# A recurrent mixer by chunks of 64 tokens with affine maps of the state, instead of chunks of 128 with a three-product chain

## The reference

```python
def wkv7_scan(r, w, k, v, a, b):
    def step(state, inp):
        r_t, w_t, k_t, v_t, a_t, b_t = inp
        sa = jnp.einsum('bhvk,bhk->bhv', state, a_t)
        state = (state * w_t[:, :, None, :] + sa[..., None] * b_t[:, :, None, :]
                 + v_t[..., None] * k_t[:, :, None, :])
        return state, jnp.einsum('bhvk,bhk->bhv', state, r_t)
...
    y = wkv7_scan(rh, wh, kh, vh, -kk, kk * ah)
    mu = jnp.mean(y, axis=-1, keepdims=True)
    var = jnp.mean(jnp.square(y - mu), axis=-1, keepdims=True)
    y = ((y - mu) * lax.rsqrt(var + GN_EPS)).reshape(B, S, C) * gn_w + gn_b
```

## Time and profile before

| | |
|---|---|
| median of 3 runs | 3302.31 us (3301.39 to 3302.34) |
| profiled execution, its own time | 3304.38 us |
| its span | 3302.4 us |
| PE, DVE, ACT, POOL busy | 96%, 52%, 32%, 60% |
| recurrent section | from about 243 to 783 us |
| mean distance of passes 1 to 7 (first products of round 1) | 60.8 us |

### The profile page before, as it was taken

How to read it: one execution, slowest core, us unless ns; L and a number is a source line. 1 busy time by engine, 2 the same in 40 slices (tenths; PEclk the granted TensorE clock), 3 DMA queues, 4 the chain that set the end, 5 groups by cost and what they waited for, 6 DMA issues and landing times.

```text
span 3302.4 us, 54354 instructions
## 1 busy us (share of the span) xinstructions
PE 3173.8 (96%) x19314; PEld 2521.1 (76%) x19314; DVE 1703.5 (52%) x2741; ACT 1066.7 (32%) x1988; POOL 1972.7 (60%) x2607
## 2 busy tenths in 40 slices
PE   6998999999999999899999999999999999999999
PEld 4766777777888888577778888887667777888887
DVE  4456777765554335542645554446551635565345
ACT  2153434432221113542635321113552535331112
POOL 4624333336588885246465888886327373898886
PEclk8999999999999999999999999999999999999999
DMA  5341111112233232112121322232102121223322
GB/s 210 138 163 51 46 40 40 40 34 77 93 98 100 95 96 65 32 52 83 40 82 58 96 96 96 95 96 83 45 27 95 46 83 46 93 93 100 98 95 96
DMA packets 70794, 265.22 MB, mean 80 GB/s; under 512 B 7744, under 2 KB 7872, under 8 KB 67520
## 3 DMA queue, kind: packets, MB, share of 16 engines
q1 hardware_dynamic: 68288, 257.59, 23.7%
q10 hardware_dynamic: 2304, 4.83, 0.4%
HBM read 260.29 MB, written 2.10 MB: 79 GB/s over the span
## 4 chain that ended last, share of the span: by engine, by line
PE 83%; DVE 9%; ACT 5%; issue 1%; DMA 1%; SPq 0%; DVEq 0%; ACTq 0%
PE psum_a L579 10%; PE psum_a L583 10%; PE psum_a L582 10%; PE psum_d L579 7%; PE psum_d L583 6%; PE psum_d L582 6%; PE psum_d L645 5%; PE psum_a L737 3%; PE psum_d L840 2%; PE psum_a L767 2%; PE psum_a L771 2%; PE psum_a L770 2%; PE psum_a L608 1%; PE psum_a L611 1%; PE psum_a L612 1%
## 5 line engine op out<-in xcount | busy, mean ns | idle before, releaser
L3383 POOL TENSOR_TENSOR w_lo<-raw,w_hi 128x256 fp32r<-128x256 f32 x1736 | 1425.7, 852 | 36.3
L3377 POOL TENSOR_TENSOR mark<-mark 128x1 f32<-128x1 f32 x432 | 105.2, 244 | 1248.0 <-PE psum_a L579 627.7
L579 PE MATMUL psum_a<-h_hi,w_hi 128*128 128x512 f32 x1600 | 631.9, 395 | 0.0
L583 PE MATMUL psum_a<-h_hi,w_lo 128*128 128x512 f32 x1600 | 623.7, 390 | 0.0
L582 PE MATMUL psum_a<-h_lo,w_hi 128*128 128x512 f32 x1600 | 623.3, 390 | 0.0
L3378 POOL TENSOR_SCALAR w_hi<-raw 128x1024 fp32r<-128x1024 f32 x434 | 459.6, 1059 | 33.3 <-DMA raw<-in_weights 33.3
L579 PEld LDWEIGHTS psum_a<-h_hi,w_hi 128*128 128x128 f32 x1600 | 300.8, 188 | 71.7 <-issue 10.7
L582 PEld LDWEIGHTS psum_a<-h_lo,w_hi 128*128 128x128 f32 x1600 | 300.9, 188 | 63.2 <-issue 2.2
L583 PEld LDWEIGHTS psum_a<-h_hi,w_lo 128*128 128x128 f32 x1600 | 300.7, 188 | 63.2
L579 PE MATMUL psum_d<-split,w_hi 128*128 128x512 f32 x848 | 329.9, 389 | 0.0
L582 PE MATMUL psum_d<-split,w_hi 128*128 128x512 f32 x848 | 329.9, 389 | 0.0
(11 more groups left out here) (407 smaller groups left out, 5524.7 us busy)
## 6 DMA issues: line engine op xcount, KB each, us to landing
raw<-in_weights SPq DMA_DIRECT2D x434, 512.0 KB, 3.4
plain<-in_ada SPq DMA_DIRECT2D x20, 1024.0 KB, 6.9
arena<-in_ada SPq DMA_DIRECT2D x4, 1024.0 KB, 16.9
x<-in_x SPq DMA_DIRECT2D x1, 2048.0 KB, 12.2
x<-in_x ACTq DMA_DIRECT2D x1, 2048.0 KB, 9.9
out<-x SPq DMA_DIRECT2D x8, 256.0 KB, 3.5
arena<-in_pe ACTq DMA_DIRECT2D x2, 512.0 KB, 3.6
const<-in_const ACTq DMA_DIRECT2D x1, 906.0 KB, 8.5
```

Source lines behind the costliest of these rows:

```text
L579: m = pe.eng.matmul(dst, wh, hi(t), start=t == 0, stop=False)
L583: m = pe.eng.matmul(dst, wl, hi(t), start=False, stop=t == k - 1)
L3377: eng.tensor_tensor(b.mark[:, 1:2], b.mark[:, 0:1], b.mark[:, 0:1], ALU.add)
L3383: m = eng.tensor_tensor(lo[:, part], b.raw[:, s, part], hi[:, part].bitcast(F32), ALU.subtract)
```

## The change

Chunks become 64 tokens, eight per head; there is no step from 64 to 128 tokens. Per chunk the state update becomes an affine map S' = E(P S + Q), and the output R' S + Y0; P, Q, R' and Y0 don't depend on the state and are made for all chunks at once. In PE's order:

- `inputs` between g2 and gate: 16 products of 128 columns (inverse times A and times K·V), copied by ACT. `maps` between gate and branch: one group of 16 products of 128 columns, two groups of 32 products of 64 columns (two terms each). DVE makes P, R' and Q (`dve_rwkv_transitions`), ACT copies Y0.
- `pe_rwkv_start` and the halves become two `pe_units` groups of 16 64-column products, masks of 256 columns instead of 512.
- The chain is six `step`s of two 64x64x64 products, two each in rounds 1 to 3, each followed by one DVE operation of 64 columns. In round 4 `outputs`: 14 products of 64 columns, and on DVE an addition of 448 columns and a copy of 64.
- The tail has the transposes, one group of 16 products of 64 columns (B, R), one of 128 columns (K, A and R), copies of A by 16 products with the identity, four transposes of the inverse, and a group of 16 (K·V). The maps' masks are two of 256 and two of 512 columns.
- The turned values go to ring "d"; DVE reduces them over the channels (8 sums per token row) and subtracts the mean while it takes them (`dve_rwkv_values`). The product for the mean of y (`pe_rwkv_mean`) and DVE's centring go.
- The log decay is one scan over 512 tokens, reset by a zero in a vector of ones at each chunk's start, and no middle is subtracted: two exponentials of 512 columns instead of eight of 128 and two small ones. Three memsets prepare the constants.
- After pass 7: gate, `inputs`, gate, `maps`, two gates with three steps each, `outputs`, gate, variance. Gates 3 to 6 go to ring "a" and are taken by ACT with the sigmoid, without DVE's copy.

The core of the diff:

```diff
-    pe_rwkv_start(pe, lambda r, c: b.R_BH[r, c * P:(c + 1) * P], lambda r, c: AR[r, c, 0])
...
+    if chain:
+        chain.inputs()
     pe_features(pe, "a", "gate", H)
+    if chain:
+        chain.maps()
     pe_features(pe, "d", "branch", of(b.s_hi, b.s_lo, 2), 2)
     pe.eng.wait_ge(pe.sem["rk_ready"], pe.due("rk_ready"))
     pe_plain(pe, "d", b.pair, b.R_T)
+    pe_units(pe, "d", (B, A))
+    pe_units(pe, "d", (A, B))
...
+        if chain and k <= 3:
+            chain.step(2 * k - 1)
+        if chain and k == 4:
+            chain.outputs()
...
-        if k == 5:
-            if j:
-                pe_rwkv_mean(pe)
-        if c is not None:
-            chain.second(c)
...
+        normal = pe_units(pe, "d", (block(b.R_TW), block(b.R_Z)))
+        if chain and k <= 3:
+            chain.step(2 * k)
         if k == 3 and more:
             pe_rwkv_length(pe)
...
+    pe_turned(pe, [b.R_V[:, q * P:(q + 1) * P] for q in range(NQ)], "d")
+    for src in (b.R_BH, b.R_KH):
+        turned = pe_turned(pe, [src[:, q * P:(q + 1) * P] for q in range(NQ)])
+    pe_units(pe, "d", (B, R))
+    maps = pe_units(pe, "d", (K, lambda v, row, out: AR[ROWS[row], 2 * v + out]), width=P)
+    pe_own_rows(pe, "a", lambda r, c: AR[r, c, 0], lambda r, c: b.ident[r, r], range(8))
     pe.eng.wait_ge(normal.free, pe.taken(normal))
...
+    inverse = pe_turned(pe, [b.R_TN[:, 2 * v:2 * v + 2].rearrange("p u t -> p (u t)") for v in range(4)])
+    pe.eng.wait_ge(turned.free, pe.taken(turned))
+    pe.eng.wait_ge(maps.free, pe.taken(maps))
+    values = pe_units(pe, "a", (block(b.R_KA[:, :, 0]), block(b.R_VN)))
```

The new helpers:

```diff
+def pe_units(pe, ring, *terms, width=HD):
+
+    tiles = [pe.tile(ring) for _ in range(2)]
+    pe.eng.wait_ge(tiles[1].free, pe.emptied(tiles[1]))
+    for v in range(4):
+        for k, (lhsT, rhs) in enumerate(terms):
+            for n, (row, out) in enumerate(((0, 0), (1, 1), (0, 1), (1, 0))):
+                m = pe.eng.matmul(tiles[row].ps[ROWS[out], v * width:(v + 1) * width], lhsT(v, row, out), rhs(v, row, out),
+                                  start=k == 0, stop=k == len(terms) - 1)
...
+    def step(self, c):
+
+        pe, b = self.pe, self.b
+        pe.eng.wait_ge(self.state.free, pe.taken(self.state))
+        tl = self.state = pe.tile("d")
         pe.eng.wait_ge(tl.free, pe.emptied(tl))
...
+        for r in ROWS:
+            m = pe.eng.matmul(tl.ps[r, 0:HD], b.R_PR[r, c, 0], self.states(c)[r], start=True, stop=True)
+        m.then_inc(tl.full, pe.up("full_d"))
...
+def dve_rwkv_values(v):
...
+    v.eng.tensor_reduce(b.R_MEAN, ps, AX, ALU.add).then_inc(v.sem["dve_step"], v.up("dve_step"))
+    v.eng.wait_ge(v.sem[v.last], v.own())
+    v.eng.scalar_tensor_tensor(b.R_VN, b.R_MEAN.unsqueeze(2).to_broadcast([P, 8, HD]), -1.0 / HD, ps, ALU.mult, ALU.add)\
         .then_inc(v.sem["free_d"], v.up("free_d"))
```

More of the change, by code:

```diff
@@ L1155, in pe_rwkv_start, with block @@
[L1155 to L1177, removed]
+def block(t):
+    return lambda v, row, out: t[ROWS[row], 2 * v + out]
@@ L1528, in pe_program @@
         chain = pe_rwkv(pe, j, chain)
-    for c in range(NQ):
-        chain.first(c)
-        tl = pe.tile("d")
-        pe.eng.wait_ge(tl.free, pe.emptied(tl))
-        pe_product(pe, tl.ps, "gate", *H, KD, None, part=range(0, 4))
-        chain.second(c)
-        pe_product(pe, tl.ps, "gate", *H, KD, None, part=range(4, KD)).then_inc(tl.full, pe.up("full_d"))
-        chain.third(c)
-    pe_features(pe, "a", "gate", H)
-    pe_rwkv_mean(pe)
+    pe_features(pe, "a", "gate", H)
+    chain.inputs()
+    pe_features(pe, "a", "gate", H)
+    chain.maps()
+    for first in (1, 4):
+        tl = pe.tile("a")
+        pe.eng.wait_ge(tl.free, pe.emptied(tl))
+        for n in range(4):
+            m = pe_product(pe, tl.ps, "gate", *H, KD, None, part=range(2 * n, 2 * n + 2))
+            if n < 3:
+                chain.step(first + n)
+        m.then_inc(tl.full, pe.up("full_a"))
+    chain.outputs()
+    tl = pe.tile("a")
+    pe.eng.wait_ge(tl.free, pe.emptied(tl))
+    pe_product(pe, tl.ps, "gate", *H, KD, None).then_inc(tl.full, pe.up("full_a"))
     pe_rwkv_variance(pe)
@@ L1754, in act_rwkv @@
         act_late_gate(a, 0)
-    for k in range(1, NQ + 2):
-        a.eng.wait_ge(a.sem["full_a"], a.due("full_a"))
-        a.eng.wait_ge(a.sem[a.last], a.own())
-        a.eng.activation(b.R_TW, a.bank().rearrange("p (u t) -> p u t", u=8), ACT.Copy).then_inc(a.sem["free_a"], a.up("free_a"))
-        if k > NQ:
-            continue
-        if j:
-            act_rwkv_chunk(a, W)
+    for k in range(1, 6):
+        act_rwkv_taken(a, b.R_TW)
         if k == 2 and more:
@@ new lines, in dve_rwkv_transitions @@
+def dve_rwkv_transitions(v, j):
+    b, AR, eye = v.b, v.b.R_AR[j % 2], v.each(v.b.const[:, C_EYE:C_EYE + HD], 4)
+    for row in range(2):
+        v.eng.wait_ge(v.sem["full_d"], v.due("full_d"))
+        ps = v.units(P)
+        v.eng.wait_ge(v.sem[v.last], v.own())
+        v.eng.tensor_tensor(other_rows(b.R_PR[:, :, 0], row), ps[:, :, 0:HD], eye, ALU.add)\
+            .then_inc(v.sem["dve_step"], v.up("dve_step"))
+        v.eng.wait_ge(v.sem[v.last], v.own())
+        v.eng.tensor_tensor(other_rows(b.R_PR[:, :, 1], row), ps[:, :, HD:], other_rows(AR[:, :, 1], row), ALU.add)\
+            .then_inc(v.sem["free_d"], v.up("free_d"))
+    ends = b.R_E[j % 2].rearrange("p (v o) -> p v o", o=2)
+    for row in range(2):
+        v.eng.wait_ge(v.sem["full_d"], v.due("full_d"))
+        v.eng.wait_ge(v.sem[v.last], v.own())
+        v.eng.tensor_tensor(other_rows(b.R_EQ, row), v.units(HD), ends[:, :, row].unsqueeze(2).to_broadcast([P, 4, HD]), ALU.mult)\
+            .then_inc(v.sem["free_d"], v.up("free_d"))
@@ L2617, in dve_rwkv @@
         level = v.each(b.const[:, C_LEVEL + (k - 1) * HD:C_LEVEL + k * HD], 4)
-        for half in range(2):
+        for row in range(2):
             v.eng.wait_ge(v.sem["full_d"], v.due("full_d"))
             v.eng.wait_ge(v.sem[v.last], v.own())
-            v.eng.tensor_tensor(every(b.R_Z, half), four(v.bank()), level, ALU.mult).then_inc(v.sem["free_d"], v.up("free_d"))
+            v.eng.tensor_tensor(other_rows(b.R_Z, row), v.units(HD), level, ALU.mult).then_inc(v.sem["free_d"], v.up("free_d"))
+        if j and k <= 3:
+            dve_rwkv_state(v, j - 1, 2 * k - 1)
+        if j and k == 4:
+            dve_rwkv_outputs(v)
         if k == 1:
```

404 lines of the change are left out of this document (149 added, 255 removed).

## The result

The changed kernel takes 3327.2 us (median of 4 runs, 3326.6 to 3327.8) where the kernel before takes 3302.3 on the same chip: a ratio of 1.007, 95% interval 1.0058 to 1.0082, so it is slower. Forecast were 3306 with a range of 3288 to 3324; the time lies 3 us outside. One execution of the later run e6_local_late took 9803 us at a granted clock of 1.00 and is left out of its ratio; its four others took 3287.7 to 3293.5. The profiled execution has a span of 3325.7 us at a mean granted clock of 0.977 (before: 3302.4 at 0.99).

The account below looks back on a forecast made before the run. The section looked bound by PE, but round 4 and nearly round 1 by DVE. Terms at unchanged clock gave -16.4, clock falls +14.4 and +6.0, sum +4.0 on 3302.31: 3306 us, range 3288 to 3324.

Parts of the forecast that it names:

- entry: Start of the section: PE's 4.01 us wait for DVE's scans and ACT's exponentials shrinks; -4.5, bounds -3 and -5.3.
- pass 0 to 1: Stretch from pass 0 to pass 1: 26.4 us becomes 27.4 plus the same slow 1.5, +2.5.
- six periods, unchanged clock: Six middle passes: period 60.7, less 0.85 for the shorter last front, 363.3 against 364.7 us, -1.4.
- six periods, falls in round 4: Round 4, PE idle 3.7 us in one piece: a clock fall in each of six passes, 2.4 each, +14.4.
- six periods, falls in round 1: Idle PE in round 1: four clock falls in seven passes, 1.5 us each, +6.0; +5.1 for the six periods.
- last pass (with its fall): Rounds of the last pass: 32.3 us becomes 28.9, -3.4 at unchanged clock; -2.5 with its fall.
- end: After the last pass's rounds, to the variance product: 52.3 us becomes 42.7, -9.6.
- The clock: Prediction step pricing clock falls from idle PE: +14.4 in round 4 and +6.0 in round 1.
- The round-by-round sum: Per pass: five doubling steps of the triangular inverse (rounds) 32.0 us, tail and front 28.7, period 60.7.
- The state step: Chain step of two concurrent products on PE: 0.11 us by its columns, taken as 0.25.
- The third: Rival: PE starves in short pieces, three more falls in round 1 and seven in round 3; 3321, slower, chance 0.30.
- The second rival: The clock holds: three of six falls in round 4 and all in round 1 stay away; 3293, faster, chance 0.25.

Follow-up runs that it names:

- e6_local_late: e3_fill_both with the local part of the outputs moved from the next pass's front to round 1, filling there cut from four products to two: 3291.2 us.
- e3_fill_both: Changed kernel plus unused PE products, four after round 1's second products and eight after round 4's: 3296.4 us, ratio 0.998.
- e2_fill4: Changed kernel plus eight unused PE products behind the second products of round 4, passes 0 to 6: 3305.2 us, ratio 1.0008.
- e11_moves_no_fill: Changed kernel with the local part moved to round 1 and output work behind round 4's second products and additions, no unused products: 3296.8 us, ratio 0.9972.
- e8_mean_back: e3_fill_both with the group norm's mean product restored and the values only copied, not centred: 3290.1 us, ratio 0.9954.
- e10_mean_back_alone: Changed kernel without any filling, with the mean product restored and the values only copied: 3316.2 us, ratio 1.0032.
- e5_outputs_late: e3_fill_both with output work moved behind round 4's second products (PE) and additions (DVE), filling there cut from eight products to six: 3289.0 us, ratio 0.9957.

## Why the prediction was wrong

The spans give +23.3 us; +4.0 was forecast. By the prediction's own terms (starts of rounds in the two timelines; the rows above and the earlier trace rows are samples of them):

| term | forecast | measured |
|---|---|---|
| entry (0.3 of it ahead of the section) | -4.5 | -2.3 |
| rounds of pass 0 | 0 | +1.6 |
| pass 0 to 1 | +2.5 | +3.5 |
| six periods, unchanged clock | -1.4 | +2.5 (by e3_fill_both) |
| six periods, falls in round 4 | +14.4 | +13.9 |
| six periods, falls in round 1 | +5.1 | +13.4 |
| last pass (with its fall) | -2.5 | -1.5 |
| end | -9.6 | -8.8 |
| outside the section | 0 | +0.9 |

The last two rows of the periods are the changed kernel less e3_fill_both: six times 0.80 + 1.52 in round 5, tail and front, and six times 2.24 in round 2.

**The step that failed** is the second half of "The clock": "I count four falls in seven, each half as long as that of pass 0 ... 4 x 1.5". The clock fell in all eight passes and cost 2.1 us each (10.00 - 8.43 in pass 0, 2.24 in the mean of the six, 1.5 in pass 7): 16.5 us instead of 6, which is 10.5 of the 19.3 that the forecast missed. Both factors were off, the count by 6 us and the price by 4.5. The price of 1.5 was right in passes 0, 2, 5 and 7 (1.4 to 1.6, granted clock of the round 0.83 or 0.84); in passes 1, 3, 4 and 6 the same instructions lost 2.2 to 2.9 (0.78 to 0.72). The count was off because I argued from one row, pass 0 of the kernel before, which idled 1.79 us before round 2 and held. In the changed kernel pass 0 stands at the same point after 1.80 us and fell; e2_fill4 and e11_moves_no_fill, whose instructions up to there are those of the changed kernel, held again (8.44 us). One pass that holds is no proof that the next does.

**The clock's other half** was right in place and size: a fall in each round 4 after the long idle piece, 13.9 for 14.4.

**The round-by-round sum** was right to 0.5 us in 60.7 (table above): round 4 is 0.34 longer, 0.2 of it since the output work takes 1.1 rather than 0.9, and round 2 is 0.26 longer. Times six, and with the 0.85 that I took off for the last front and that the trace doesn't give back, that makes 3.8 us. The state step was priced at 0.25 and not at its 0.11 of columns. Neither is its price everywhere. Behind 64x64 products it adds 0.10 (from round 3's second products to the length product 0.73 us, 419.53 to 420.26; without a step, in pass 0, 0.63, 290.25 to 290.88). Between transposes and feature in round 2 it adds 0.44 (e3_fill_both: 0.85 in pass 2, 397.65 to 398.50, against 0.41 in pass 0, 278.02 to 278.43). The Trainium skill, "TensorEngine Tiling (Array Packing)", Key Properties, says that a change of tiling mode drains the array; the trace agrees, since the step is dear where it stands between two groups of 128x128.

**The entry** gave less than half. From the last rows ahead of the section (PE, 240.75 before and 240.46 now) to round 1 it takes 33.35 instead of 35.39 us, 2.0 less. PE's wait was to be under 1 us and is 2.27; its timeline answers to the earlier trace rows:

```profile
263.60 1.13 PE L646 MATMUL psum_d<-arena,const 128*128 128x512 f32 x2 [2.27 <-DVE arena L2469]
```

Scan and exponentials shrank as forecast (the one scan took 1.22), but the next product waits for DVE's preparation of pass 0, so a part of the time saved at ACT is handed on to DVE. Behind that wait the clock fell too: the window from 264 to 270 stands at 0.72. In e3_fill_both, e8_mean_back and e11_moves_no_fill, whose instructions up to there are the same, it stands at 1.00, and the stretch takes 32.2 us. So 1.1 of the missing 2.5 is the clock; that the rest is DVE's row I only argue.

**The rivals.** The third, PE starving in short pieces (3321, chance 0.30), was nearest and right about round 1, wrong about round 3 in the changed kernel: with idle pieces of 0.95 and 0.42 its window stands at 1.00. In six of the later kernels the clock did fall in round 3, though in one or two passes of eight, and not in seven. The rule of the Trainium skill ("TensorE: Matmul & The Clock Gate", "A second HAM failure mode: psum-queue depth-cycling") said that short idling between groups makes the clock swing; the trace agrees for the pieces of 1.8 to 3.4 us before round 2 of the changed kernel, and for the short ones of round 3 only in those later kernels. The second rival, that the clock holds (3293, 0.25), is what e3_fill_both made of it, at 3296.

## What to carry to other kernels

Work taken out of pieces in which PE otherwise idles isn't only worth nothing: where it was what kept PE's clock up, removing it costs time later (2.1 us a pass in round 2 here), so a change that makes an engine's share smaller must be priced with the clock at both levels, once per place and for all passes. If a place idles, move work into it that counts elsewhere, as the local group of e11_moves_no_fill, before filling it with unused products. And before a product is traded for work on another engine, look whether the product waited beside something: here the mean product lay in a wait for ACT, and the centring that replaced it lies in one that PE feels.

## What the runs showed of the hardware

- One and the same stretch of instructions held the full clock in two runs and lost it in two others (round 2 of pass 0: 8.44 us in e2_fill4 and e11_moves_no_fill, 10.00 in the changed kernel and in e10_mean_back_alone, with 1.80 us of idle time ahead of it in the changed kernel). The idle piece alone doesn't decide. Round 2 held after 2.08 us in two passes of e10_mean_back_alone and after 2.45 in e11_moves_no_fill, and fell after 2.09 in the changed kernel; round 3 fell after pieces of 1.31 and 0.42 in e5_outputs_late.
- A fall's price isn't fixed: over the same instructions of round 2, with a feature of 24 matmuls in it, it was 1.4 to 2.9 us in one execution, and for round 5, tail and front 2.3 in the mean.
- Two 64x64x64 products cost 0.10 us behind other 64x64 products and 0.44 between two groups of 128x128 (rounds 3 and 2).
- PE's timeline has gaps with no releaser ("issue") of 0.2 to 1.0 us, at other places in each run, for instance 0.96 in the middle of a gate feature of e3_fill_both at 752.20. That is one part of the spread between runs of one kernel. Another is that the recurrent section doesn't start at the same time: its last row ahead of it stands at 236.57 us in e2_fill4 and at 240.66 in e3_fill_both, after the same instructions.
